# One-hot rows written token by token and read contiguously, and a wait for each of the last units

## The reference, cut to what matters

```python
    def block(xb):
        q = (xb @ w_query).reshape(PEER_TOKEN_BLOCK, PEER_HEADS, 2, D_KEY // 2)
        s = jnp.einsum('thpc,pkc->thpk', q, sub_keys).astype(jnp.float32)
        s1, i1 = lax.top_k(s[:, :, 0], PEER_TOPK)
        s2, i2 = lax.top_k(s[:, :, 1], PEER_TOPK)
        cand = (s1[..., :, None] + s2[..., None, :]).reshape(PEER_TOKEN_BLOCK, PEER_HEADS, PEER_TOPK * PEER_TOPK)
        sc, ci = lax.top_k(cand, PEER_TOPK)
        e = (jnp.take_along_axis(i1, ci // PEER_TOPK, axis=-1) * N_KEYS
             + jnp.take_along_axis(i2, ci % PEER_TOPK, axis=-1))
        g = jax.nn.softmax(sc, axis=-1)
        u = expert_u[e]
        act = jax.nn.gelu(jnp.einsum('td,thkd->thk', xb, u).astype(jnp.float32))
        return jnp.einsum('thk,thkd->td', (g * act).astype(xb.dtype), expert_v[e])
```

## Time and profile before

| | |
|---|---|
| median of 3 runs | 1370.74 us (1369.51 to 1370.87) |
| profiled execution | 1368.58 us, its span 1366.8 us |
| TensorE matmuls busy | 1316.4 us, 96% |
| VectorE busy | 943.5 us, 69% |
| ScalarE busy | 690.4 us, 51% |
| f16 matmuls (L916) | 512, 70.7 us busy |

### The profile page before, as it was taken

The page is one execution under the profiler, slowest core; times in us unless marked ns, Lnnn a source line. Parts: engine busy times, 40 slices in busy tenths (PEclk is TensorE's granted clock), DMA queues, the critical chain, the costliest instruction groups (busy, mean ns, idle before and its releaser), DMA issues.

```text
span 1366.8 us, 22018 instructions
## 1 busy us (share of the span) xinstructions
PE 1316.4 (96%) x8592; PEld 1200.9 (88%) x8592; DVE 943.5 (69%) x1792; ACT 690.4 (51%) x1135; POOL 33.1 (2%) x27
## 2 busy tenths in 40 slices
PE   7999998999989899999999999999999999999996
PEld 6889978998877678999999999999988888888885
DVE  5765676674456755999899666676667676767665
ACT  5566456664455744444454444444444545454553
POOL 0000130000020000000000000000000000000000
PEclk9999999999999998999999999999999999999999
DMA  7533455666646335477767655555567676766763
GB/s 241 165 122 111 141 171 155 184 184 187 194 147 195 126 102 174 145 237 228 228 218 237 190 169 170 185 171 157 169 225 264 234 245 234 248 249 239 244 235 106
DMA packets 72662, 260.55 MB, mean 191 GB/s; under 512 B 8224, under 2 KB 8864, under 8 KB 72304
## 3 DMA queue, kind: packets, MB, share of 16 engines
q1 hardware_dynamic: 71520, 255.77, 57.7%
q0 software_dynamic: 1040, 3.38, 0.8%
HBM read 240.25 MB, written 18.87 MB: 190 GB/s over the span
## 4 chain that ended last, share of the span: by engine, by line
PE 87%; DVE 5%; ACT 4%; DMA 2%; issue 1%; SPq 0%; DVEq 0%; ACTq 0%
PE ps L933 24%; PE ps L453 14%; PE ps L461 13%; PE ps L462 13%; PE ps L463 13%; PE ps L916 4%; ACT whi L968 1%; PE ps L496 1%; DVE wlo L1396 1%; DVE mg L1654 1%; DMA raw<-in_expert_v_dram 1%; PE ps L471 1%; DMA raw<-in_w_in_dram 1%; PE ps L477 1%; DMA X<-in_x_dram 1%
## 5 line engine op out<-in xcount | busy, mean ns | idle before, releaser
L1396 DVE TENSOR_TENSOR wlo<-raw,whi 128x1024 fp32r<-128x1024 f32 (+2 forms) x410 | 498.0, 1216 | 352.8 <-ACT whi L968 350.7
L968 ACT ACTIVATE whi<-raw 128x1024 fp32r<-128x1024 f32 (+2 forms) x421 | 441.5, 1050 | 443.6 <-PE ps L463 166.0
L461 PE MATMUL ps<-TH,whi 128*128 128x256 f32 x1536 | 443.3, 289 | 2.3 <-DVE TL L1405 1.2
L462 PE MATMUL ps<-TL,whi 128*128 128x256 f32 x1536 | 436.3, 284 | 0.0
L463 PE MATMUL ps<-TH,wlo 128*128 128x256 f32 x1536 | 435.8, 284 | 0.0
L461 PEld LDWEIGHTS ps<-TH,whi 128*128 128x128 f32 x1536 | 296.9, 193 | 3.2 <-issue 3.0
L462 PEld LDWEIGHTS ps<-TL,whi 128*128 128x128 f32 x1536 | 296.3, 193 | 0.0
L463 PEld LDWEIGHTS ps<-TH,wlo 128*128 128x128 f32 x1536 | 295.7, 193 | 0.0
L933 PE MATMUL ps<-whi,TH 128*128 128x512 f32 x512 | 199.5, 390 | 5.2 <-DVE wlo L1396 3.7
L933 PE MATMUL ps<-whi,TL 128*128 128x512 f32 x512 | 199.2, 389 | 0.0
L933 PE MATMUL ps<-wlo,TH 128*128 128x512 f32 x512 | 199.2, 389 | 0.0
(11 more groups left out here) (292 smaller groups left out, 1365.3 us busy)
## 6 DMA issues: line engine op xcount, KB each, us to landing
raw<-in_expert_u_dram SPq DMA_DIRECT2D x128, 512.0 KB, 3.7
raw<-in_expert_v_dram SPq DMA_DIRECT2D x128, 512.0 KB, 3.6
raw<-in_w_up_dram SPq DMA_DIRECT2D x32, 512.0 KB, 3.7
raw<-in_w_down_dram SPq DMA_DIRECT2D x32, 512.0 KB, 4.3
acts<-stage SPq DMA_DIRECT2D x32, 512.0 KB, 4.1
stage<-acts SPq DMA_DIRECT2D x30, 512.0 KB, 3.3
raw<-in_w_in_dram SPq DMA_DIRECT2D x20, 512.0 KB, 4.3
raw<-in_w_gate_dram SPq DMA_DIRECT2D x16, 512.0 KB, 3.5
```

The costliest lines, as they stand in the source:

```text
L461: e.matmul(dst, whi[:, h, sl], xh[:, k, :], start=k == 0, stop=False)
L462: e.matmul(dst, whi[:, h, sl], xl[:, k, :], start=False, stop=False)
L968: e.activation(whi[:, u % NH, 0:n], raw[:, u % NR, 0:n], ACT.Copy).then_inc(*hi(u))
L1396: e.tensor_tensor(wlo[:, u % NH, 0:n], raw[:, u % NR, 0:n], whi[:, u % NH, 0:n].bitcast(F32), ALU.subtract).then_inc(*lo(u))
```

## The change

Two edits. First, `room` has its last two axes swapped, so that each token's one-hot is a contiguous row of 128 f16, and `one_hots` writes it token by token: a comparison of `keys` (now each key number once) with the token's i1, and twice a comparison with its i2 that is multiplied by g_hi or g_lo in the same instruction. i1, i2, g_hi and g_lo are read as one value for each partition. A group has 12 such instructions in place of 4, and the wait of VectorE for its own comparison (`hot_key`) is gone. Second, of the last three units the first two are waited for one by one, each ahead of its own matmuls for t=0, and the last one after those.

```diff
-        keys = sb(p4, "keys", [128, 128, 4], F16)
+        keys = sb(p4, "keys", [128, 128], F16)
-        room = X[:, :, :]...rearrange("p (s w k t) -> p s w k t", s=2, w=3, t=4)
+        room = X[:, :, :]...rearrange("p (s w t k) -> p s w t k", s=2, w=3, t=4)
@@ tensor_program
-                            m = e.matmul(ps[g % 4][:, i * 128:i * 128 + 128], room[:, g % 2, 0, :, i], room[:, g % 2, w, :, i],
+                            m = e.matmul(ps[g % 4][:, i * 128:i * 128 + 128], room[:, g % 2, 0, i, :], room[:, g % 2, w, i, :],
                                          start=w == 1, stop=w == 2)
...
-            for n in range(125, 128):
+            for n in range(125, 127):
                 whole(EV + n)
                 e.wait_ge(*cut_d.at(n))
-            for n, d in ((125, 0), (125, 1), (126, 0), (126, 1)):
-                accumulate(n, 0, d)
+                for d in range(2):
+                    accumulate(n, 0, d)
+            whole(EV + 127)
+            e.wait_ge(*cut_d.at(127))
@@ vector_program
-            e.tensor_copy(keys[:, :, :], bc(cs("iota"), 2, 4))
+            e.tensor_copy(keys[:, :], cs("iota")).then_inc(*route_d("keys"))
...
             def one_hots(g):
-                s, ts = g % 2, slice(4 * g, 4 * g + 4)
-                h1, h2, h2_low = (room[:, s, w, :, :] for w in range(3))
                 if g >= 2:
                     e.wait_ge(*weighed.at(g - 2))
-                e.tensor_tensor(h2_low, keys[:, :, :], bc(i2T[:, ts], 1, 128), ALU.is_equal).then_inc(*hot_key(g))
-                e.tensor_tensor(h1, keys[:, :, :], bc(i1T[:, ts], 1, 128), ALU.is_equal)
-                e.wait_ge(*hot_key.at(g))
-                e.tensor_tensor(h2, h2_low, bc(g_hi[:, ts], 1, 128), ALU.mult)
-                e.tensor_tensor(h2_low, h2_low, bc(g_lo[:, ts], 1, 128), ALU.mult).then_inc(*hot(g))
+                for i in range(4):
+                    first, second, second_low = (room[:, g % 2, w, i, :] for w in range(3))
+                    at = slice(4 * g + i, 4 * g + i + 1)
+                    e.tensor_scalar(first, keys[:, :], i1T[:, at], None, ALU.is_equal)
+                    e.tensor_scalar(second, keys[:, :], i2T[:, at], g_hi[:, at], ALU.is_equal, ALU.mult)
+                    m = e.tensor_scalar(second_low, keys[:, :], i2T[:, at], g_lo[:, at], ALU.is_equal, ALU.mult)
+                m.then_inc(*hot(g))
```

More of the change, by code:

```diff
@@ L249, in build @@
         g_lo = sb(p4, "g_lo", [128, 256], F16)
-        keys = sb(p4, "keys", [128, 128, 4], F16)
+        keys = sb(p4, "keys", [128, 128], F16)
         stage = sb(p4, "stage", [128, 8, 256])
-        room = X[:, :, :].rearrange("p t n -> p (t n)").bitcast(F16)[:, 0:3072].rearrange("p (s w k t) -> p s w k t", s=2, w=3, t=4)
+        room = X[:, :, :].rearrange("p t n -> p (t n)").bitcast(F16)[:, 0:3072].rearrange("p (s w t k) -> p s w t k", s=2, w=3, t=4)
         gb4, squares, fin = raw[:, 0, :], raw[:, 1, :], raw[:, 2:4, :]
@@ L422, in build @@
         last_d = signal("last_d", ["00", "10", "01", "11"])
+        route_d = signal("route_d", ["keys", "ex", "done", "turned1", "turned2"])
         routed = signal("routed", range(1, 99))
-        route_d = signal("route_d", ["ex", "done", "turned1", "turned2"])
         query_d = signal("query_d", [1, 3, 5, 7, 9, 11, 13, 15])
         score_d = signal("score_d", range(4))
-        hot_key = signal("hot_key", range(64))
         hot = signal("hot", range(64))
@@ L2022, in vector_program @@
                         e.wait_ge(*route_d.at("turned2"))
+                        e.wait_ge(*route_d.at("keys"))
                         e.wait_ge(*d_kept.at(0))
```

## The result

The changed kernel takes 1356.12 us (median of 4 runs, 1354.57 to 1356.52) against 1370.18 us for the kernel before (4 runs): 14 us less, a ratio of 0.9913 with a 95% interval of 0.9895 to 0.9931. I had forecast 1345, some 25 us less. The direction was right, the size about half; the time measured lies 3 us from the first rival's 1359, "VectorE becomes the bound because each per-partition operand is paid".

The account below looks back on a forecast made before the run. TensorE was taken to bound the kernel. From 1368.58 us, -23.9 (groups) + 1.0 (first two groups) - 2.6 (end) = -25.5 gave 1343.1; the median, 2.2 above, 1345. Range 1336 to 1373, leaving out the third rival.

Parts of the forecast that it names:

- the first rival: VectorE's one-hots: each per-partition operand is paid, 2.5 us a group, VectorE sets a period of 3.65 us; 1359 us, chance 0.17.
- the value taken for VectorE: VectorE's twelve one-hot instructions a group: 0.168 us each, second operand read beside the first, 2.0 us together.
- "more" bound: VectorE's one-hots: 0.06 us paid again for a second operand, 4 x 0.168 + 8 x 0.23 = 2.5 us a group.
- So 2.0 is hidden: VectorE's 3.14 us of work fits in a unit with a group of 3.44 us, with 0.3 us left.
- the first two groups: Two groups back to back at unit 66: the second's inputs come later, f32 work resumes at 771.3, loss 1.0 us.
- TensorE's term: TensorE's f16 matmuls with contiguous operands: a group takes 0.57 us, 0.385 less, 23.9 us over 62 groups.
- the extra 0.05 us for the step back to f32: TensorE's return to f32 after a group: grows by 0.05 us that a shorter f16 matmul no longer hides of a load.
- The argument for the moving operand: TensorE's f16 matmuls: the moving operand's step, not the weight load, sets 0.107 us a pair; contiguous, 0.054.
- the second rival: TensorE's f16 matmuls: the weight load, or anything but the stride, sets 0.107 us, period stays; 1369.5 us, chance 0.13.
- The end: The last units: matmuls of units 125 and 126 fill TensorE's wait, what follows moves 2.6 us earlier.
- final_norm_g's load: Near the end: lands at 1354.8, in time by 0.5 us for the multiply that would move to 1355.3.
- The third rival: VectorE's new instructions miss the f16 rate: 2.8 to 3.6 us a group, 1379 to 1429 us, chance 0.15.

Follow-up runs that it names:

- one_operand: The changed kernel with the constant 0.5 in place of g_hi and g_lo in the comparisons of i2: 1338.61 us, ratio 0.9792 to the kernel before.
- moving_contig: The kernel before with only the f16 matmuls' moving operand read contiguously, VectorE's instructions untouched, weights table not computed: 1336.47 us.
- stationary_contig: The kernel before with only the f16 matmuls' stationary operand read contiguously, the moving one with step 4, weights table not computed: 1368.89 us.
- tail_only: The kernel before with only the second edit, the waits for the last three units: 1364.65 us against 1367.04, ratio 0.9977.
- after_again: The changed kernel run once more as yardstick, beside the kernel before on the other version's chip: 1351.06 us, ratio 0.9883.
- mixed_layout: The changed kernel, complete, with the stationary one-hot written as before, four tokens by one instruction, only the moving ones token by token: 1339.67 us, ratio 0.9798.

## Why the prediction was wrong

**The step that failed** is the value taken for VectorE: "I take this for all twelve, the second operand's read beside the first: 2.0 us." The price for one operand was right, 0.168 forecast, 0.162 measured in one_operand and 0.16 to 0.17 in the changed kernel, and so was the f16 rate, taken from two-tensor instructions. But the second operand is not read beside the first. It costs another 0.06 us, and eight of twelve instructions have one: 4 x 0.165 + 8 x 0.223 = 2.44 us, which was my "more" bound of 2.5. The rows had priced the first operand at 0.06 us, and nothing in them said that a second would be free; I chose between the two prices without a row that told them apart, with 0.3 us of slack hanging on it. "So 2.0 is hidden" then fell with it: 1.13 + 2.44 = 3.57 us is more than TensorE's 3.38, and it is the period that the chain shows to the hundredth. Of 3.83 - 3.38 = 0.45 us that TensorE gained in a unit, VectorE lets 0.255 through. one_operand shows this directly, as the time follows when that operand alone is taken away.

**What I left out.** Three units have two groups, and I priced only the first. Today the others cost TensorE 0.955 us more than a plain one; now they take 1.13 + 4.88 = 6.01 us (6.02 in the chain), 1.24 more than the 4.78 before. With that the stretch adds up: 58 units by 0.255 us are 14.8 saved, less 2 x 1.24, less 1.75 at the first two groups (first one-hot to f32 work 5.45 us, before 3.7), is 10.6, against 10.1 read from the trace. My first rival had the mechanism: the first groups lose 2.0 (1.75 found) and the end gives 2.6 (2.9 found). Its period of 3.65 was 0.08 too long, 5 us over the stretch, and the 2.5 us of the two crowded units, which it leaves out too, took half of that back: 1359 in place of 1356. That it came so near is in part luck.

**TensorE's term** was right in its mechanism, and its gain a little small: 0.57 us a group forecast, 0.51 measured (3.38 less 2.87). The half rate at step 1 (0.054 us a pair) was exact, and the extra 0.05 us for the step back to f32 was not needed. The argument for the moving operand (a long matmul record, a short load record, equal bytes) is confirmed by moving_contig and stationary_contig, and the second rival is out. The rule of the Trainium skill that I weighed there ("SBUF — State Buffer", section "Door 1: The DMA port swizzle", the note on SBUF cachelines), by which 2-byte numbers may be read up to eight apart at full rate, and four apart too, is not what TensorE does in these runs: step 4 doubles the time, and step 3 already makes 0.74 of 0.48 us. The 81 ns a pair of the Trainium skill's "TensorE: Matmul & The Clock Gate", section "Back-to-back issue gap", is not met either; the pairs here take 54 ns.

**The end** was right, mechanism and size: -2.6 forecast, -2.9 in the table above, -3.1 (-1.2 to -5.1) alone in tail_only. final_norm_g's load was in time.

**The third rival** (VectorE without the f16 rate) did not happen: 24 f32 columns cost 0.14 us and 128 f16 ones 0.162.

## What to carry to other kernels

When an edit speeds up the engine that bounds, compute the other engines' work against the new, shorter period, unit by unit and for the crowded units too; if a gain rests on less slack than the spread of one unmeasured price, the likelier forecast is the dearer price that the nearest rows show. Count each operand that VectorE reads per partition as about 0.06 us of an instruction, a third of a short one; for the second operand one_operand shows it, for the first it is worked out from the earlier trace rows and no run takes it away. Before a layout is changed for both operands, try them apart: here one of them gave all of it, and leaving the other alone is what turned 16 us into 27.6 on one chip (after_again and mixed_layout).

## What the runs showed of the hardware that I had not expected

The step of a moving f16 operand costs from more than 4 bytes a column on, about in proportion to the bytes passed over (0.48, 0.51, 0.74, 0.955, 1.85 us for eight at 2, 4, 6, 8, 16 bytes), while the stationary operand's step of 8 bytes costs 0.02 to 0.03 us a group.

At the unit with two groups near 917 us TensorE stood still for 1.81 us, and its clock then fell for some 3 us. Windows of the changed kernel (length, busy PE, PEld, DVE, ACT, POOL, clock, DMA, GB/s):

```profile
770.00:774.00 4.00, 3.43 (x26) 3.44 (x27) 4.00 (x17) 1.82 (x3) 0.00 (x0) 0.76 0.25 82
...
844.00:848.00 4.00, 3.40 (x32) 3.34 (x32) 4.00 (x16) 1.82 (x3) 0.00 (x0) 1.00 0.33 76
...
916.00:920.00 4.00, 2.15 (x21) 1.94 (x21) 4.00 (x17) 1.26 (x3) 0.00 (x0) 0.85 0.14 55
920.00:924.00 4.00, 4.00 (x31) 3.96 (x30) 4.00 (x16) 1.15 (x2) 0.00 (x0) 0.72 0.43 133
```

The mean clock is 0.85 and 0.72 of full there, which is part of the time at 1.2 GHz instead of 2.4; f32 matmuls start 0.21 us apart in place of 0.12. It cost nothing: TensorE came late, VectorE's one-hots got ahead of it meanwhile, and TensorE then ran seven units at its own 3.38 us until the lead was used up. That is the stretch from 923.56 us on in the chain above. VectorE's splits kept their 3.57 to 3.58 us all the while. After the same wait of 1.81 us at the first two groups the clock fell too (0.76 in the first window); it made one of VectorE's splits come 0.1 us late. After the one near 843 us it did not fall. In after_again it fell near 917 us alone. So the same wait brings a fall in some places and executions and not in others, and what decides these runs leave open.
